# Interleaving light and heavy attention units of one mixer in a two-layer streaming encoder

## What is computed

```python
z = x @ w_in                       # q_A | k_A | v_A | c_q | c_kv | k_rope
yA = windowed attention, 8 heads in 2 key groups, window 128, chunk 64, sink and relative bias
yB = latent attention over c_kv (all 512 keys; for streams 512 cached keys + 16 new)
g = sigmoid(x @ w_gate + b_gate)
h = g[:D] * (yA @ w_proj_a) + g[D:] * (yB @ w_proj_b)
x = LN1(alpha * x + h @ w_out)
x = LN2(alpha * x + ConvGLU(x))
```

```python
s = q @ k.T * SWA_SCALE + bias
m = max(max(s), sink)
p = exp(s - m); p = p / (sum(p) + exp(sink - m))
y = p @ v
```

## Time and profile before

| what | value |
|---|---|
| median of 3 runs | 1906.08 us (1904.06 to 1906.64) |
| the profiled execution, its own time | 1906.51 us |
| its span, first to last instruction | 1904.7 us |
| TensorE clock granted, mean | 0.993 |
| PE busy | 1856.2 us, 97% of the span |
| DVE, ACT, POOL busy | 53%, 35%, 28% |
| DMA | 169 MB, 89 GB/s over the span |

### The profile page before, as it was taken

One profiled execution on the slowest core, in us unless ns is written; L12 is line 12 of the kernel. 1 busy time (PEld: TensorE's weight loads), 2 busy tenths in 40 slices (PEclk: granted clock), 3 DMA queues, 4 the chain that ended last, 5 costly groups with the idle time before them and its releaser, 6 DMA issues. The chain is left out here.

```text
span 1904.7 us, 32034 instructions
## 1 busy us (share of the span) xinstructions
PE 1856.2 (97%) x12530; PEld 1763.7 (93%) x12530; DVE 1011.9 (53%) x1597; ACT 660.5 (35%) x1392; POOL 542.8 (28%) x240
## 2 busy tenths in 40 slices
PE   8899999999999999999999999999999999999996
PEld 8887888899999999999998888879999999999995
DVE  3457544458854332443785765444697443234447
ACT  3236333532442312332342443334334332133323
POOL 2232111134143244332422312112322332433331
PEclk9899999999999999999999999999999999999998
DMA  6442232332122123111341513313321211222121
GB/s 181 122 118 84 95 122 82 113 122 89 45 89 79 53 69 109 66 60 53 102 129 48 155 54 129 103 65 134 106 77 67 88 56 67 77 89 77 52 74 56
DMA packets 59091, 169.45 MB, mean 89 GB/s; under 512 B 8152, under 2 KB 26248, under 8 KB 51272
## 3 DMA queue, kind: packets, MB, share of 16 engines
q1 hardware_dynamic: 58984, 167.97, 26.6%
HBM read 149.42 MB, written 18.28 MB: 88 GB/s over the span
## 5 line engine op out<-in xcount | busy, mean ns | idle before, releaser
L674 POOL TENSOR_TENSOR w_lo<-w_raw,w_hi 128x1024 fp32r<-128x1024 f32 (+2 forms) x234 | 537.0, 2303 | 1326.7 <-ACT w_hi L748 1307.6
L748 ACT ACTIVATE w_hi<-w_raw 128x1024 fp32r<-128x1024 f32 (+2 forms) x232 | 221.3, 972 | 473.9 <-PE ps L1582 441.7
L1582 PE MATMUL ps<-x_hi,w_hi 128*128 128x320 f32 x1408 | 323.3, 311 | 5.2 <-POOL w_lo L674 3.0
L1582 PE MATMUL ps<-x_lo,w_hi 128*128 128x320 f32 x1408 | 322.4, 310 | 0.0
L1582 PE MATMUL ps<-x_hi,w_lo 128*128 128x320 f32 x1408 | 322.2, 310 | 0.0
L1582 PEld LDWEIGHTS ps<-x_hi,w_hi 128*128 128x128 f32 x1408 | 236.9, 189 | 6.1 <-issue 3.5
L1582 PEld LDWEIGHTS ps<-x_lo,w_hi 128*128 128x128 f32 x1408 | 237.1, 189 | 0.0
L1582 PEld LDWEIGHTS ps<-x_hi,w_lo 128*128 128x128 f32 x1408 | 236.8, 189 | 0.0
L1482 DVE TENSOR_SCALAR f_conv<-f_ext,vec 128x656 f32<-128x656 f32 x44 | 63.9, 1452 | 202.6 <-ACT tail L971 200.2
L1852 PE MATMUL ps<-x_hi,w_hi 128*128 128x320 f32 x512 | 163.5, 319 | 1.3 <-ACT logits L836 1.3
L1852 PE MATMUL ps<-x_hi,w_lo 128*128 128x320 f32 x512 | 158.3, 309 | 0.0
(11 more groups left out here) (278 smaller groups left out, 3208.5 us busy)
## 6 DMA issues: line engine op xcount, KB each, us to landing
w_raw<-in_slabs SPq DMA_DIRECT2D x84, 1024.0 KB, 4.8
w_raw<-in_slabs SPq DMA_DIRECT2D x20, 768.0 KB, 4.0
gate_logits<-logits SPq DMA_DIRECT2D x64, 160.0 KB, 1.8
gates<-gate_logits SPq DMA_DIRECT2D x16, 640.0 KB, 6.5
w_raw<-in_slabs SPq DMA_DIRECT2D x16, 640.0 KB, 3.8
ckvc<-in_ckvc SPq DMA_DIRECT2D x16, 256.0 KB, 2.7
ckvc_t<-in_ckvc_t SPq DMA_DIRECT2D x16, 256.0 KB, 3.0
w_raw<-in_slabs SPq DMA_DIRECT2D x6, 512.0 KB, 5.7
```

Source lines behind the costliest of these rows:

```text
L674: pool.tensor_tensor(to, w_raw[:, s % 2, c], hi.bitcast(F32), ALU.subtract).then_inc(wlo_ready, 1)
L748: A(w_hi[:, s % 2, c], w_raw[:, s % 2, c], ACT.Copy).then_inc(whi_ready, 1)
L1582: ins = MM(out_[:, a, :], w, x[:, t, a * HT:(a + 1) * HT], start=t == 0 and w is wh and x is hi, stop=t == tiles - 1 and w is wl)
```

## The change

The order of mixer A's 16 units is another. Before, units 0 to 7 are the prompt's and 8 to 15 the streams'. After, units 0 to 2 are the prompt's first three, then streams 0 to 4 and the prompt's other five alternate (streams at 3, 5, 7, 9, 11, prompt at 4, 6, 8, 10, 12), and units 13 to 15 are streams 5 to 7. Mixer B's units keep their numbers 16 to 39, and `AS_LAST` stays 15. Where the code asked whether a unit is one of the first 8, it now asks for its kind.

```diff
-UNITS = [("Ap", i, g) for i in range(NB) for g in range(GH // 2)] + [("As", r, 0) for r in range(NREQ)]
+
+PROMPT_A = [("Ap", i, g) for i in range(NB) for g in range(GH // 2)]
+STREAM_A = [("As", r, 0) for r in range(NREQ)]
+UNITS = PROMPT_A[:3] + [x for two in zip(STREAM_A, PROMPT_A[3:]) for x in two] + STREAM_A[len(PROMPT_A) - 3:]
...
-NAP = sum(x[0] == "Ap" for x in UNITS)
...
+assert B_FIRST == AS_LAST + 1
+
+
+def copied_by_two(u):
+
+    return sum(x[0] != "Ap" for x in UNITS[:u + 1])
+
...
-                    if u < NAP:
+                    if UNITS[u][0] == "Ap":
                         A(*turned_copy(u, 1), ACT.Copy)
                     A(*turned_copy(u, 0), ACT.Copy).then_inc(turned_act, 1)
...
-                    if u >= NAP:
+                    if UNITS[u][0] != "Ap":
                         turned_half(u)
...
-                    if u >= NAP:
-                        pe.wait_ge(turned_dve, layer * (NU - NAP) + u - NAP + 1)
+                    if UNITS[u][0] != "Ap":
+                        pe.wait_ge(turned_dve, layer * copied_by_two(NU - 1) + copied_by_two(u))
```

## The result

The changed kernel takes 1912.39 us (median of 6 runs, 1910.64 to 1913.49) against 1905.19 us before (6 runs, 1904.06 to 1907.55): ratio 1.0033, 95% interval 1.0023 to 1.0043. It is slower by more than the 0.2% that can be told from no change. The profiled execution took 1910.70 us over a span of 1908.9 us, with PE busy for 1857.4 us (97%) and a mean granted clock of 0.992.

What follows compares the result with a forecast made beforehand. PE, busy for 97% of the span, was taken as the bound. Waits of 2.8 us for two layers (-0.9 + 0.6 + 1.7 each) plus 1.7 for one clock fall gave 1911.0 profiled, 1910.6 us by the median; range 1905.9 to 1914.4.

Steps and rivals of the forecast that it cites:

- Turn(4): Mixer A, PE's turn of unit 4, no gate piece ahead: lost time falls from 1.43 to 0.53 us, gain 0.9 per layer.
- E: Start on PE of the values behind the last gate piece, from which the prediction counts each turn's time.
- Turn(12): Mixer A, PE's turn of unit 12: lost time grows from 0.60 to 1.15 us, cost 0.6 per layer.
- Turn(8): Mixer A, turn of unit 8: POOL's subtraction blocks DVE ahead of a heavy normalise; cost 1.7 us per layer.
- The clock: PE's clock behind turn(8): one fall to 0.50 in the two layers, some 3.4 us long, worth 1.7 us.
- the rival with falls in both layers: PE's clock falls behind turn(8) in each layer, 2.8 + 3.4 us: 1912.3 us; chance 0.25.
- The sum of the turns' waits: PE's turns waiting for DVE's probabilities, 6.9 us before: total near 9.5 us after the change.
- over 0.5 us of slack: Turns in places with a gate piece: they have this slack, so their beginning to wait would prove the prediction wrong.
- The cache of the streams: First stream's scores, now unit 3, wait for `kc_t` and `vc`: some 4 us of other work hides it, zero cost.
- waits grow, the clock holds: Rival: PE's waits grow by 2.8 us among the units without a fall of the clock: 1908.9 us; chance 0.24.
- no block: Rival: POOL does not block DVE at unit 8, so turn(8) waits as turn(4) does: 1904.7 us; chance 0.13.
- the waits vanish: Rival: light units shorten DVE's queue so heavy ones are never late, 6.1 us gained: 1900.0 us; chance 0.05.

Runs made afterwards that it cites:

- The hold experiments: POOL's subtraction behind gate piece 7 held until turn(8) is done: on the changed kernel 1904.91 us, on the kernel before 1904.72 us.
- The heavy-3 run: Changed kernel with units 3 and 4 exchanged, so a heavy (prompt) unit stands at place 3: 1909.37 us, ratio 1.0018 to the kernel before.
- 2.49 us in the old order: Kernel before with eight more small maxima on DVE ahead of normalise(8), so that only turn(8) waits longer: 1910.30 us, ratio 1.0023.
- the run with the hold: Changed kernel with POOL's subtraction behind gate piece 7 held until turn(8) is done: 1904.91 us, ratio 0.9999 to the kernel before.

## Why the prediction was right

It said 1910.6 us, between 1905.9 and 1914.4, slower with a chance of 0.57. The time was 1912.39, 1.8 us above the forecast, the sign and in the main the mechanism as forecast. Point by point:

- **Turn(4)**: forecast 3.90 us behind E, measured 164.71 - 160.79 = 3.92. The wait in brackets, which is some 0.1 to 0.2 less than the "lost" of the prediction's sums, went from 1.36 to 0.37: the gain of 0.9 was 1.0.
- **Turn(12)**: forecast 4.05 behind E, measured 207.00 - 202.92 = 4.08; the cost of 0.6 was 0.55 (0.46 to 1.01). The heavy unit that waits was the right reason.
- **Turn(8)**: forecast POOL's end at E + 4.3 and the turn at E + 6.2. With E = 180.76, POOL ended at E + 4.39 and the turn came at E + 6.12, and turn(8) waited 2.42 us. The cost of 1.7 was 1.5. Which DVE operation would be held was left open between L1200 and the next one. It was the next: L1209 (the old L1200) started 0.04 us before POOL and ran its 0.16 us, and L1210 was held to POOL's end. By the rule cited from the Trainium skill ("SBUF — State Buffer", section "Who interferes with whom") POOL should then have started later by what the DVE operation had left, 182.93 - 182.81 = 0.12 us. The trace does not show that: POOL's record starts within L1209's and is no longer than before, 2.34 against 2.36 us. It agrees on the rest, that the second DVE operation is held to POOL's end. The hold experiments confirm the term: without the block the whole loss is gone.
- **The clock**: forecast one fall of 3.4 us, worth 1.7; each profile showed one, of 3.4 us, worth 1.5. Giving the fall a price at all was what brought the forecast near, since waits alone make 3 us of the 7. Over all executions the granted clock speaks for 1.4 to 1.7 falls, between the forecast's one and the two of the rival with falls in both layers (1912.3), to which 0.25 was given and whose time the median matched. The forecast's ground, that 2.2 us sufficed ahead of the units, was a single case: over the thirteen profiles that place has a fall with waits of 2.2, 2.2, 2.6, 3.1, 3.1 and 3.6 us and none with waits of 2.4 and 2.5.
- **The sum of the turns' waits**: "near 9.5 us" was 10.2. The step that failed is the last sentence of the prediction: turns in gated places have "over 0.5 us of slack". Turn(1) began to wait, 0.63 and 0.61 us, which was a stated sign of being wrong and is a term of 1.2 us that the sum had at nothing. That the sum came out near is in part luck: the three places that were worked out cost 2.1 us together in place of 2.8 (-2.0 + 3.0 + 1.1, by the waits in brackets), and turn(1) made up for it, 3.3 in all. The kernel before shows why it should have been worked out like the other three; its timelines of DVE and PE:

```profile
148.88 0.87 DVE L1222 TENSOR_SCALAR probs<-probs,st_ri 128x128 f32<-128x128 f32 x4
```

```profile
149.80 0.66 PE L1786 MATMUL ps<-ident,probs 128*128 128x128 f32 x4
```

  Normalise(1) ended at 148.88 + 0.87 = 149.75 and turn(1) started at 149.80: no slack at all. It had no wait in brackets only because heavy scores(3) filled the time to the last 0.05 us. With light scores, some 0.5 us in place of 1.13, the difference became a wait. A turn without a wait was taken for a turn with slack. (DVE is held by POOL there too, for 1.2 us in both kernels.) The heavy-3 run took this wait away, and turn(4)'s, and measured 1.4 us less, within the noise of two runs.
- **The cache of the streams**, `kc_t`, is covered, as said: no row of PE waits for it.

Of the rivals, "waits grow, the clock holds" is excluded by the clock's rows, "no block" by the 2.20 us of L1210, "the waits vanish" by four turns that wait in each layer.

## What to carry to other kernels

Ahead of a change of order, work out the slack of every place where a filler stage ends, those without a wait too: a wait of nothing is not slack. Put the long member of a pair where the other engines' chain is not itself behind; better still, spread filler so that no place is without it: in the old order and in a partly interleaved one that gained 4 to 6 us, more than any order did. It helps only where the engines behind have time to catch up; in the full interleaving, filler at one place took 1.71 us from turn(8) and gave 1.29 back one piece later. Price a growing idle time of TensorE twice, once as waiting and once as matmuls at half clock behind it.

## What was not expected of the hardware

- Keeping PE busy with useless matmuls made the kernel faster. 20 transposes of the identity, 2.40 us in place of idle time and ended before the data came, took the time from 1910.80 to 1907.07 us.
- The same wait lets the clock fall or not: 2.42 to 2.44 us of idle PE, twice per execution in three profiles, gave three falls in six places, once in layer 1 and twice in layer 0; 2.49 us in the old order gave none behind it in two, while waits of 0.73 and 0.57 us amid short matmuls, in the same execution, were each followed by one.
- POOL blocks only some of DVE's work. In the run with the hold, DVE's maximum over 128x1024 scores in PSUM took 1.22 us beside POOL's subtraction, as long as ever, and the operation of 128x4 numbers in SBUF behind it was held until POOL had ended, 0.02 us apart.
